# Expert weights in 64 KB rows and 8 MB loads in a decoder block with a mixture of experts

## What is computed

```python
def moe_ffn(h, w_router, b_router, w_gate, b_gate, w_up, b_up, w_down, b_down):
    logits = (h @ w_router + b_router).astype(jnp.float32)
    top_val, top_idx = lax.top_k(logits, TOP_K)              # TOP_K = 4 of 32
    gates = jax.nn.softmax(top_val, axis=-1).astype(h.dtype)
    ...
    def expert_block(args):
        xb, e = args
        g = xb @ w_gate[e] + b_gate[e]                       # each weight is 1024 x 1024
        u = xb @ w_up[e] + b_up[e]
        g = jnp.minimum(g, SWIGLU_LIMIT)
        u = jnp.clip(u, -SWIGLU_LIMIT, SWIGLU_LIMIT)
        glu = g * jax.nn.sigmoid(SWIGLU_ALPHA * g)
        return ((u + 1.0) * glu) @ w_down[e] + b_down[e]
```

## Time and profile before

| | us |
|---|---|
| median of 3 runs | 1102.84 (1102.41 to 1103.43) |
| the profiled execution: span from the first to the last instruction | 1100.7 |
| PE busy in it | 1042.3 (95%) |
| DVE busy / ACT busy | 302.7 / 130.8 |
| loads of 4096 KB, 77 of them, median from issue to landing | 47.7 |
| loads of experts of 2048 KB, 28 of them, median from issue to landing | 13.1 |

### The profile page before, as it was taken

How to read it: one execution, slowest core, us unless ns; L and a number is a source line. 1 busy time by engine, 2 the same in 40 slices (tenths; PEclk the granted TensorE clock), 3 DMA queues, 4 the chain that set the end, 5 groups by cost and what they waited for, 6 DMA issues and landing times.

```text
span 1100.7 us, 12887 instructions
## 1 busy us (share of the span) xinstructions
PE 1042.3 (95%) x5458; PEld 500.9 (46%) x5458; DVE 302.7 (28%) x622; ACT 130.8 (12%) x243; POOL 13.1 (1%) x18
## 2 busy tenths in 40 slices
PE   9999999999999999999999989989898979998896
PEld 8999996534433443344342423433243323332332
DVE  5977888420302111121111111211102020302022
ACT  2212250310000001001000100001000000000012
POOL 1200000000000000000000000000000000000000
PEclk9999999999999999999999999999999999999999
DMA  8974377999999999999999999999999999999996
GB/s 327 427 304 154 145 294 291 358 422 428 431 433 432 430 433 432 430 433 432 430 433 432 430 433 432 430 433 432 430 433 432 430 433 432 430 433 432 425 427 261
DMA packets 26799, 438.17 MB, mean 398 GB/s; under 512 B 5008, under 2 KB 6416, under 8 KB 9616
## 3 DMA queue, kind: packets, MB, share of 16 engines
q1 hardware_dynamic: 26192, 435.05, 93.4%
q10 hardware_dynamic: 576, 2.69, 0.6%
HBM read 436.28 MB, written 1.05 MB: 397 GB/s over the span
## 4 chain that ended last, share of the span: by engine, by line
PE 61%; DMA 35%; DVE 1%; SPq 1%; issue 1%; ACT 1%; another core or an unknown queue 1%; DVEq 0%; POOL 0%; POOLq 0%
DMA ring<-in_experts 35%; PE ps L2073 24%; PE ps L2122 12%; PE ps L1632 8%; PE ps L1983 3%; PE ps L2131 3%; PE ps L1811 2%; PE ps L1627 2%; PE ps L1876 2%; PE ps L1681 1%; PE ps L2111 1%; PE ps L1992 1%; SPq L507 1%; ACT region_va L855 0%
## 5 line engine op out<-in xcount | busy, mean ns | idle before, releaser
L2073 PE MATMUL ps<-ring,xT 128*64 128x512 f32 x2044 | 456.9, 602 | 27.5 <-DMA ring<-in_experts 27.5
L2073 PEld LDWEIGHTS ps<-ring,xT 128*64 128x64 f32 x2044 | 143.7, 138 | 313.3 <-issue 281.6
L2122 PE MATMUL ps<-ring,region_va 128*64 128x512 f32 x1024 | 227.9, 595 | 21.8 <-DMA ring<-in_experts 11.1
L2122 PEld LDWEIGHTS ps<-ring,region_va 128*64 128x64 f32 x1024 | 72.9, 137 | 155.1 <-issue 126.5
L1527 DVE TENSOR_SCALAR g<-ps 128x1024 f32<-128x1024 f32 x16 | 19.6, 1225 | 349.7 <-PE ps L2073 343.8
L1632 PE MATMUL ps<-ring 128*128 128x128 f32 x784 | 89.7, 276 | 0.1
L1632 PEld LDWEIGHTS ps<-ring 128*128 128x128 f32 x784 | 88.5, 192 | 0.9 <-DVE ring L941 0.3
L1473 DVE TENSOR_TENSOR xT<-ps,g_ffn 128x512 f32<-128x512 f32 x30 | 20.8, 692 | 190.9 <-PE ps L1983 190.9
L1549 DVE TENSOR_SCALAR region_va<-ps 128x512 f32<-128x512 f32 x32 | 22.1, 692 | 179.8 <-PE ps L2073 179.8
L1983 PEld LDWEIGHTS ps<-sel,x 128*128 128x128 f32 x480 | 55.4, 192 | 9.5 <-issue 9.5
L2131 PE MATMUL ps<-g,g_T 128*128 128x512 f32 x128 | 59.2, 605 | 0.0
(11 more groups left out here) (271 smaller groups left out, 533.9 us busy)
## 6 DMA issues: line engine op xcount, KB each, us to landing
ring<-in_experts SPq DMA_DIRECT2D x77, 4096.0 KB, 47.7
ring<-in_experts SPq DMA_DIRECT2D x28, 2048.0 KB, 13.1
ring<-in_head SPq DMA_DIRECT2D x13, 2048.0 KB, 16.5
ring<-in_experts SPq DMA_DIRECT2D x13, 1024.0 KB, 9.1
ring<-in_first SPq DMA_DIRECT2D x7, 384.0 KB, 6.6
ring<-in_experts SPq DMA_DIRECT2D x5, 512.0 KB, 9.5
ring<-in_experts ACTq DMA_DIRECT2D x2, 1024.0 KB, 9.6
ring<-in_experts SPq DMA_DIRECT2D x1, 1536.0 KB, 6.0
```

The lines of the kernel that those rows point to most:

```text
L2073: last = mm(bank(banks + half)[rows, :], xT[:, 2 * m + c, rows], weights[:, k], start=False, stop=m == 3 and c == 1, skip_group_check=True)
L2122: last = mm(bank(first + half)[rows, :], hTm[:, 2 * m + c, rows], w[:, c, half, k], start=m == 0 and c == 0, stop=m == 3 and c == 1, skip_ ...
```

## The change

The memory layout: the block of a matrix is now 128 rows of 64 KB, so that a whole matrix of a pair (8 MB) is one load with one row for each partition. Loads of a slot, a unit or a piece take columns of these rows.

- Pairs 3 to 12: three loads of 8 MB each (`load_matrix`), asked for when TensorE has used the last slot of the matrix (`used(n, 4*w + 3)`).
- Pair 2: loads 0 and 1 of 2 MB, then units 1, 2 and 3 of 4 MB, then the down matrix of 8 MB.
- Pairs 13 and 14: units of 4 MB as before. Pair 15 and pair 0: sizes as before. Pair 1: sizes as before.
- `unit_loaded[1::2]` serve as `matrix_loaded[0..2]`. In pairs 1 to 12 TensorE waits for a whole matrix ahead of its first matmul; pair 2's gate also waits for 3 x 16 of `third_parts` (loads 0, 1 and unit 2).
- TensorE's loop has six turns (pairs 1 to 12); pairs 13 and 14 are written out.

```diff
+MATRICES = 3
+LOADS_PER_MATRIX = LOADS_PER_PAIR // MATRICES
+MATRIX_COLS = LOADS_PER_MATRIX * SLOT_COLS
+WHOLE_PAIRS = 12
+LOOP_ITERS = WHOLE_PAIRS // PAIRS_PER_ITER
-SECOND_PAIR_LOADS = [5, 4, 3, 2, 2, 2]
+SECOND_PAIR_LOADS = [9, 5, 4]
+def matrix_count(n, w):
+    return (n - 1 + SECOND_PAIR_LOADS[w]) * 16
 def unit_count(n, m):
-    return (n - 1 + SECOND_PAIR_LOADS[m]) * 16
+    return matrix_count(n, m // 2) if m % 2 else (n - WHOLE_PAIRS) * 16
...
+            def load_columns(pair, p, lo, hi, loaded):
+                w, k = divmod(p, LOADS_PER_MATRIX)
+                at = k * SLOT_COLS
+                sp_.dma_start(whole(SLOT_OF[p])[:, lo:hi], experts_v[pair * MATRICES + w][:, at + lo:at + hi]
+                              ).then_inc(loaded, 16)
+            def load_unit(pair, m, loaded=None):
+                w, k = divmod(m, 2)
+                rows = experts_v[bass.ds(pair * MATRICES + w, 1)].rearrange("k p n -> (k p) n")
+                sp_.dma_start(unit(m), rows[:, 2 * k * SLOT_COLS:2 * (k + 1) * SLOT_COLS]
+                              ).then_inc(loaded or unit_loaded[m], 16)
+            def load_matrix(pair, w):
+                sp_.dma_start(matrix(w), experts_v[bass.ds(pair * MATRICES + w, 1)].rearrange("k p n -> (k p) n")
+                              ).then_inc(matrix_loaded[w], 16)
...
+            def used(n, p):
+                sp_.wait_ge(load_used, n * LOADS_PER_PAIR + p + 1)
...
+            def load_third_pair():
+                for p in range(2):
+                    used(2, p)
+                    load_columns(2, p, 0, SLOT_COLS, third_parts)
+                for m, loaded in ((1, matrix_loaded[0]), (2, third_parts), (3, matrix_loaded[1])):
+                    used(2, 2 * m + 1)
+                    load_unit(2, m, loaded)
+                used(2, LOADS_PER_PAIR - 1)
+                load_matrix(2, MATRICES - 1)
+            def load_matrices(pair, n):
+                for w in range(MATRICES):
+                    used(n, LOADS_PER_MATRIX * (w + 1) - 1)
+                    load_matrix(pair, w)
+            def load_units(pair, n):
+                for m in range(UNITS):
+                    used(n, 2 * m + 1)
+                    load_unit(pair, m)
...
-            load_iteration(None, 0)
-            load_iteration(1, 1, opening=True)
-            with sp_.Fori(2, ITERS - 1) as i:
-                load_iteration(i, i)
-            load_iteration(ITERS - 1, ITERS - 1, closing=True)
+            load_second_pair()
+            load_third_pair()
+            load_matrices(3, 3)
+            with sp_.Fori(2, LOOP_ITERS) as i:
+                for q in range(PAIRS_PER_ITER):
+                    load_matrices(i * PAIRS_PER_ITER + q, i * PAIRS_PER_ITER + q)
+            load_matrices(WHOLE_PAIRS, WHOLE_PAIRS)
+            for n in range(WHOLE_PAIRS + 1, PAIRS - 1):
+                load_units(n, n)
+            load_last_pair(PAIRS - 1, PAIRS - 1)
...
-                    elif m % 2 == 0:
+                    elif matrices and m % LOADS_PER_MATRIX == 0:
                         if m == 0 and q == 0:
-                            pe.wait_ge(third_even, 16)
-                        if m == ASIDE_LOAD - 1 and q == 1:
+                            pe.wait_ge(third_parts, 16 * 3)
+                        if m == 0 and q == 1:
                             pe.wait_ge(aside_next, 16)
+                        pe.wait_ge(matrix_loaded[m // LOADS_PER_MATRIX], matrix_count(n, m // LOADS_PER_MATRIX))
+                    elif not matrices and m % 2 == 0:
                         pe.wait_ge(unit_loaded[m // 2], unit_count(n, m // 2))
...
-            with pe.Fori(0, ITERS - 1) as i:
-                expert_pair(i * PAIRS_PER_ITER + 1, 1)
-                expert_pair(i * PAIRS_PER_ITER + 2, 0)
+            with pe.Fori(0, LOOP_ITERS) as i:
+                expert_pair(i * PAIRS_PER_ITER + 1, 1, matrices=True)
+                expert_pair(i * PAIRS_PER_ITER + 2, 0, matrices=True)
+            for n in range(WHOLE_PAIRS + 1, PAIRS - 1):
+                expert_pair(n, n % PAIRS_PER_ITER)
...
 def expert_weights(a):
-    out = np.empty((PAIRS, 3, 2, P, 4, 2, 2, W512), np.float32)
+    out = np.empty((PAIRS, MATRICES, P, KC, 2, 2, W512), np.float32)
     for w, name in enumerate(("w_gate", "w_up", "w_down")):
-        out[:, w] = a[name].reshape(PAIRS, 2, 2, 4, P, 2, W512).transpose(0, 2, 4, 3, 5, 1, 6)
-    return out.reshape(PAIRS * UNITS * P, 2 * SLOT_COLS)
+        out[:, w] = a[name].reshape(PAIRS, 2, KC, P, 2, W512).transpose(0, 3, 2, 4, 1, 5)
+    return out.reshape(PAIRS * MATRICES * P, MATRIX_COLS)
```

More of the change, by code:

```diff
@@ L177, in unit, with matrix @@
             return ring[:, 2 * m * SLOT_COLS:2 * (m + 1) * SLOT_COLS]
+        def matrix(w):
+            return ring[:, w * MATRIX_COLS:(w + 1) * MATRIX_COLS]
         def slot(s, rows, cols):
@@ L495, in _, with load_half @@
                 sp_.dma_start(whole(HEAD_SLOT[n]), head_v[n - 1]).then_inc(slot_loaded[HEAD_SLOT[n]], 16)
-            def load_half(row, p, first_pair=False):
+            def load_half(pair, p, first_pair=False):
                 m, odd = divmod(p, 2)
-                cols = slice(odd * SLOT_COLS, (odd + 1) * SLOT_COLS)
-                sp_.dma_start(whole(SLOT_OF[p]), experts_v[row][:, cols]
-                              ).then_inc(unit_loaded[m] if odd and not first_pair else slot_loaded[SLOT_OF[p]], 16)
@@ L504, in load_columns @@
[L504 to L514, removed]
+                load_columns(pair, p, 0, SLOT_COLS,
+                             unit_loaded[m] if odd and not first_pair else slot_loaded[SLOT_OF[p]])
@@ L516, in load_last @@
+            def load_matrix(pair, w):
+                sp_.dma_start(matrix(w), experts_v[bass.ds(pair * MATRICES + w, 1)].rearrange("k p n -> (k p) n")
+                              ).then_inc(matrix_loaded[w], 16)
+            def load_last(pair):
                 p = LOADS_PER_PAIR - 1
[L517 to L521, removed]
+                load_columns(pair, p, 0, SLOT_COLS // 2, last_rows)
+                load_columns(pair, p, 2 * D, 3 * D, last_left)
+                load_columns(pair, p, 3 * D, 4 * D, unit_loaded[UNITS - 1])
@@ L523, in load_last_but_one @@
+            def load_last_but_one(pair):
                 p = LOADS_PER_PAIR - 2
-                load_columns(row, p, 0, SLOT_COLS // 2, third_rows)
-                load_columns(row, p, SLOT_COLS // 2, SLOT_COLS, slot_loaded[SLOT_OF[p]])
-            def load_iteration(i, it, opening=False, closing=False):
-                for q in range(PAIRS_PER_ITER):
[L529 to L563, removed]
@@ new lines, in load_last_but_one, with load_second_pair @@
+                load_columns(pair, p, 0, SLOT_COLS // 2, third_rows)
+                load_columns(pair, p, SLOT_COLS // 2, SLOT_COLS, slot_loaded[SLOT_OF[p]])
+            def used(n, p):
+                sp_.wait_ge(load_used, n * LOADS_PER_PAIR + p + 1)
+            def load_second_pair():
+                for p in range(LOADS_PER_PAIR):
+                    loaded = matrix_loaded[p // LOADS_PER_MATRIX]
+                    if p >= HALVED:
+                        used(1, p)
+                        load_columns(1, p, 0, SLOT_COLS, loaded)
+                        continue
+                    if p == 0:
+                        sp_.wait_ge(first_rows_used, 1)
+                        load_columns(1, p, 0, D, loaded)
+                    elif p > ACT_LOADS:
+                        sp_.wait_ge(first_rows_used, p + 2)
+                        load_columns(1, p, 0, SLOT_COLS // 2, loaded)
+                    used(1, p)
+                    load_columns(1, p, SLOT_COLS // 2, ASIDE_FROM if p == ASIDE_LOAD else SLOT_COLS, loaded)
@@ new lines, in load_units, with load_last_pair @@
+            def load_units(pair, n):
+                for m in range(UNITS):
+                    used(n, 2 * m + 1)
+                    load_unit(pair, m)
+            def load_last_pair(pair, n):
+                for p in range(LOADS_PER_PAIR):
+                    used(n, p)
+                    if p == LOADS_PER_PAIR - 2:
+                        load_last_but_one(pair)
+                    elif p == LOADS_PER_PAIR - 1:
+                        load_last(pair)
+                    else:
+                        load_half(pair, p)
@@ L2015, in start_y, with expert_pair @@
                 last.then_inc(sc_done, SC_AHEAD)
-            def expert_pair(n, q, first_pair=False, last_pair=False):
+            def expert_pair(n, q, first_pair=False, last_pair=False, matrices=False):
                 first, second = pair_bank(q), pair_bank(q + 1)
```

29 lines of the change are left out of this document (16 added, 13 removed).

## The result

| | before | changed |
|---|---|---|
| median of the runs (8 of each, side by side) | 1102.39 us | 1105.01 us |
| ratio, 95% interval | | 1.0022 (1.0013 to 1.0031) |
| span of the profiled execution | 1100.7 us | 1103.0 us |
| merged loads of 8192 KB | 0 | 31 |

The changed kernel is 2.6 us slower. The forecast had it 1.1 us slower. The range holds the measured time. "No change that can be told" was given 0.66 and ended at 1105.0 us; the median of 1105.01 lies on that line, so the runs don't say on which side it falls, but the interval of the ratio leaves out 1, so it is slower than before.

A forecast was written before the change was run, and what follows sets the result against it. The load stream was taken to bound the kernel: span 1100.7 + 3.0 (dry spell) - 2.2 (saving) + 0.3 (fetches) = 1101.8 us. With the median 2.1 above the span, the forecast was 1103.9 us, range 1101.4 to 1106.6.

The forecast's parts named there:

- No change that can be told: Whole kernel: a time between 1100.6 and 1105.0 us counts as the same as before; chance 0.66.
- What bounds it: Expert stage: one unbroken load stream sets the end; TensorE counts only if still behind at about 1029 us.
- The saving: Pairs 2 to 12: 31 merged pairs of loads save 0.07 us each, 2.2 us; bounds 0 and 4.5.
- Rival (a): Merged loads: 64 KB rows are cut into pieces as today, gain 0 to 0.3, 1105.8 to 1106.1 us; chance 0.13.
- Rival (e): Expert loads: memory serves a 64 KB pitch worse, even 1% being 6 us, 1110 us; chance 0.03.
- The fit of 2.0 us a transfer: Merged loads: a skill page's fixed cost, if paid in series, would save some 60 us; the prediction rejected it.
- The dry spell: Pair 2's down, about 311 us: nothing queued, restart costs 2.5 us, 2.9 to 3.0 lost; at most 3.5, at least 0.6.
- instruction fetches: Written-out pairs 13 and 14: extra 16 KB fetches hold one DMA engine about 0.6 us; cost 0.3, bounds 0 and 0.6.
- The second dry spell: Pair 3's gate: issued 3.9 us ahead of the landing against a 2.5 us lead-in, so none occurs, by 1.4 us.
- rival (c): Pair 3's gate: the stream runs dry again, 1 to 2.5 us more, 1105 to 1106.5 us; chance 0.07.
- TensorE's waits: Pairs 1 to 14: fewer, longer waits and more half clock, back in step with 3.7 us to spare; cost nothing.
- Rival (b): TensorE after pair 12: over two low-clock spells use up the 3.7 us of room, 1105.6 to 1107 us; chance 0.07.

The follow-up runs named there:

- the fastest kernel: Kernel before with 29 matrices (from pair 3's up to pair 12) as single 8 MB loads, pair 2 and TensorE's code as before: 1100.16 us, 0.9977 of before.
- same order, 4 and 8 MB: Changed kernel with order and waits kept but each 8 MB matrix issued as two 4 MB loads: 1107.21 us, against the changed kernel's 1105.01 and 1105.23.
- 1.9 for 25: Changed kernel with pair 2's down and the gates of odd pairs 3 to 11 in two loads, 25 matrices at 8 MB: 1102.11 us, 0.9994 of before.
- the layout alone: Kernel before with only memory changed to 64 KB rows, its loads cut from them as columns: 1102.77 us, 0.9997 of before.
- the spell alone: Kernel before with the first half of pair 2's down asked for only when all of pair 1's down is done: 1106.89 us, 1.0036 of before.
- two kernels with 4 MB loads: Changed kernel with 4 MB loads, issued in its own order (1107.21 us) or as in the kernel before (1103.65 us).
- the third experiment: Changed kernel with pair 2's down in two loads and pair 12's gate held back so the stream runs dry near 860 us: 1111.22 us, 1.0075 of before.
- the written-out pairs alone: Kernel before with only TensorE's pairs 13 and 14 taken out of the loop and written out: 1104.01 us, 1.0012 of before.
- the first experiment: Changed kernel with pair 2's down in two 4 MB loads, the first asked for at half of pair 1's down: 1103.49 us, 1.0009 of before.

## Why the prediction was right, and where it was off, point by point

**What bounds it: right.** Before, after and in the fastest kernel TensorE waits 1.88 or 1.89 us for the last piece of pair 14, and what the stream lost or won by then moved the end with it: 3.6 to 4.1 us for one spell, 7.7 for the larger one with what followed it, 2.6 the other way.

**The saving: right.** 31 x 0.07 = 2.2 us; measured 2.0 to 2.2 (same order, 4 and 8 MB), 1.9 for 25, 2.6 +- 1.0 for 29. Rival (a), rows of 64 KB cut up as before, has fallen: the pace is 19.36. Rival (e) has fallen with the layout alone. The fit of 2.0 us a transfer that the prediction sets against the pace stands, in the Trainium skill's page "DMA: Bandwidth & Descriptors", in the section "Anatomy of one DMA — SWDGE (gpsimd) path" and not under Bandwidth, for transfers that GpSimd issues. That it isn't paid for each load of SyncE's full queue is what the runs show: 29 merged pairs gave 2.6 us and not 58.

**The dry spell: right in its place and cause, too small in size.** Its own lead-in, 2.5 by the working, was 2.45, 2.65 and 2.7 where no fetch fell into the stretch. Before the issue 0.7 us went by in the changed kernel and 1.1 with the spell alone, for 0.5. But 3.6 (two kernels with 4 MB loads) and 4.1 (the spell alone) were paid in time and not 3.0, and in the changed kernel's own landings the spell is 23.8 - 19.4 = 4.4 us. That is more than the 3.5 the prediction gave as its most. The landings put the rest on the fetch that follows: 10.9 for 9.71 with one in the stretch. The expectation ahead of the third experiment, that 1.1 us belongs to a fetch and not to large rows, held.

**The term that failed: instruction fetches.** The prediction gave them 0.3 and at most 0.6, as the time that 16 KB take on one engine, for the code of the written-out pairs. But the packet of one fetch takes 0.96 us, the written-out pairs alone cost 1.5 us (0.3 to 2.3), and behind a spell a fetch that the kernel before has too moved a landing by 1.1 to 1.5 us, or by 0.2 to 0.7 two loads further. The picture behind it is that a load lands with its slowest engine, so that a fetch on an engine that is ahead doesn't show, and the prediction took that for the rule. That this is why the sizes differ from case to case is argued and not shown. Against a clean split into "level after a spell" and "out of step else" speaks the layout alone, where one fetch moved a landing by 1.2 us without any spell; and the same fetch in two executions of the changed kernel moved one by 0.2 and by 0.7. No run moved a fetch to another time.

**The second dry spell: right, but by a narrow path.** Pair 3's gate is issued 3.9 us ahead by the working, 5.2 in the profile (329.8 against the landing at 335.0), so rival (c) didn't come about. But it had room only because the first spell had already made the stream late. With that removed, the same issue was 1.0 us ahead, and the stream ran dry there. The prediction worked this out for the changed kernel; the expectation of the first experiment didn't do so for its own.

**TensorE's waits: right.** Longer idle time, more half clock, back in step in pair 14 (predicted some 2 us of waits, seen 2.03 and 1.89), and no cost. Rival (b) has fallen. That half-clock time ahead of the tail is free held in the fastest kernel too.

**The sum.** With the terms that the experiments measured: 3.6 for the spell, 0.8 for code and coarse waits, less 2.2, is 2.2 us; measured 2.6 with an interval of 1.4 to 3.4. The changed kernel's own landings divide it otherwise: 4.4 for the spell, 0.2 for the next load but one, less 2.1 for the other 30 merged pairs, 2.5 us, and nothing for the written-out code. That fits the last piece of pair 14, which starts 2.87 later, 0.5 of which was there before the spell (311.2 for 310.7). Three fetches fall between pair 12's down and the last piece of pair 14 (915.8 to 1032.3 us), and yet (1032.3 - 915.8) / 12 = 9.71 us for each 4 MB:

```profile
q8 instruction: 3, 0.05, 0.2%
```

So the 0.3 us that the forecast put on this code isn't there in that execution, and the fetch whose landing came late is one that the kernel before has too. The range held although the spell broke its own bound of 3.5 us; it did so because of the room left for rivals that didn't come about, and that much of it is luck.

## What to carry to other kernels

In a kernel whose end hangs on one stream of loads, put next to each load the time at which its space comes free and the landing of the load ahead of it: the issue has to lead that landing by what a restart takes over the pace (here 2.5 to 2.7 us), or the stream pays the difference. A larger load moves this time to that of its last piece, and removing one shortfall can expose the next, so the whole list has to be gone through again after each repair. And unrolling a loop is not free when the loads are the bound: one turn of two pairs written out cost 1.5 us here (0.3 to 2.3), in fetches that the profile counts on the same 16 DMA engines.

## What the runs showed of the hardware that was not expected

- A full queue moves 2 MB in 4.90, 4 MB in 9.71 and 8 MB in 19.36 us, so each load saved is worth 0.07 to 0.08 us at either step; the length of the rows doubled with the size of the loads, and no run tells the two apart. A load from an empty queue lands 2.45 to 2.7 us later than the pace, with 2, 4 and 8 MB.
- The packet of one fetch of 16 KB of code takes 0.96 us, longer than its bytes at the pace of the loads would (0.6, an estimate from 432 GB/s over 16 engines). It delayed the landing of a large load by 1.2 us (10.9 for 9.71) and, right after a restart, of another by 1.5 (20.9 for 19.35). In the undisturbed stream of the kernel before, the one fetch in the stretch from 310.7 to 330.1 us moved nothing: two loads landed in 19.4 us. With the layout alone, one in an equally undisturbed stream moved a landing by 1.2. The queues of the stretch in the kernel before are these:

```profile
q1 hardware_dynamic: 287, 8.36, 100.2%
q8 instruction: 1, 0.02, 0.3%
```

- Rows cut from a pitch of 64 KB load as fast as from one of 32 KB (0.9997, 0.9988 to 1.0006), and loads of 8 MB with a row of 64 KB in each partition have a pace a shade better than two of 4 MB with 32 KB (19.36 against 19.43 us), not worse.
